# Deeper unit pipelines, a third value buffer and dense filler products in a one-step hybrid decoder kernel

## The chip, the cores and the metric

The kernel runs on one core of one Trainium2 chip. The metric is the device time of one execution in microseconds, the median over runs. All arithmetic is in float32 except mask products and fillers, which are bfloat16.

## The reference, cut to what matters

One layer of a hybrid decoder is applied to a prompt of 512 tokens and to 8 sample tokens, with the same weights:

```python
u = rmsnorm(x);  cols = u @ w_in                      # 1024 -> 4992, 13 slabs of 384 columns
# A: 6 heads, gated linear recurrence; the samples start from a given 64x64 state per head
# B: 6 heads, differential attention, 512 prompt keys / 512 cached + 1 keys per sample
p = softmax(mask(q @ k.T) * 32 ** -0.5);  o = (p[0] - lam * p[1]) @ v
# C: 3 groups of 4 heads, windows (128, 512, 2048) with strides (1, 4, 16); groups are
#    combined in proportion to their softmax denominators
mix = concat(readout_A(oa, silu(g)), readout_B(ob), combine_C(...))
h = x + mix @ w_out
h = h + hier_moe(rmsnorm(h))      # top group of 4, top 2 of its 4 experts; 16 experts, d_ff 512
h = h + sigmoid(rmsnorm(h) @ ple_w_gate) * (p_l @ ple_w_proj)
y = rmsnorm(h)
```

The new states, keys, values and window contents are outputs as well. The samples' cached keys and values of B lie in pages, found through a page table.

## The kernel before, in words

Each engine runs its own in-order program. Up to the output projection the programs are generated from one common list of steps, made by `schedule`; each engine executes, in the list's order, those steps that it has a function for. So a step's place in the list is its place in every engine's queue, the DMA queue of SyncE (SP) among them. Engines synchronise by counting semaphores.

The stages of the list, and where they lie in the profiled execution:

- **Projection and recurrence (17 to 239 us).** `proj` steps are pieces of the combined projection (L1967, L1972, L1975, L1978): a unit is 128 columns by 512 tokens ("FM"), or 128 tokens by 256 or 384 columns ("TM"), or the 8 samples ("SM", and "SS", which sums its four partial rows). A unit is cut in 4 pieces of 2 of the 8 contraction chunks (8 x 128). Units alternate between PSUM banks 0 and 1, weight slabs between two buffers. `weave` puts pieces behind the TensorE steps of the recurrence, 1.6 for each.
- **Sample state (239 to 267 us).** Eight `dst_v` steps: TensorE broadcasts a sample's value row to 128 partitions (L2188, contraction over 8 rows), VectorE multiplies it (L1604). Pieces are woven in at 0.3 for each, four more follow, then `dst_o` (L2197).
- **Differential attention (267 to 460 us).** 24 units (4 query tiles, 6 heads), each with three steps: `d_s(n)` makes two score maps in PSUM (L2049, mask L2052), VectorE takes the maximum (L1459), ScalarE exponentiates (L993); VectorE's `weigh` forms p0 - lam p1 (L1471 to L1474); `d_t(n)` transposes (L2064) and ScalarE copies (L1003); `d_pv(n)` multiplies by the values (L2076). The list goes `d_s(n)`, `d_t(n-1)`, `d_pv(n-2)`: 72 steps. After each, 1.7 pieces of projection. Probabilities lie in two buffers, the halves of `wk`. On VectorE `d_s(n)` first weighs unit n-1 and then takes the maximum of n.
- **Cached keys.** `q_out` stores the samples' queries; `cached(b, 0)` loads sample b's keys and its query, broadcast, into one of two buffers; GpSimd multiplies them (L786 to L788); `dec_q(b)` on VectorE sums (L1544 to L1547). The first comes 11 steps after `q_out`, then one every 5. `dec_new` (L1520 to L1539) prepares selection masks and the scores of the new rows.
- **Dilated attention (460 to 546 us).** 16 units, again score (L2094, mask L2096), maximum (L1482), exponential (L1027), transposes (L2112, copy L1038), value products (L2133): `c_s(n)`, `c_t(n-1)`, `c_pv(n-2)`, 48 steps. Four dense bfloat16 products of 128x256 (L2107, `BUSY`), whose result is overwritten, go ahead of each unit's transposes. The eight "res" units store their result and softmax statistics through DRAM to reorder rows; the merge on VectorE (L1496 to L1510) needs them back. No projection piece is left here. Beside these steps, one by one: `gate_fn` (a Silu on ScalarE with two table loads, L955), `dec_soft` and `dec_norm` (softmax of the samples), `krows` 0 to 3 (key rows transposed L2151, copied to two staging buffers L1060, stored by GpSimd), `dec_wt`, `gate_mul` (L1375), 16 `dec_v` steps (products of a sample's weights with its cached values: L2216 and L2211, then VectorE L1592 and L1588), and the read-outs `ro(i)` (L1654 to L1659, with ScalarE L1081 and L1082 between). `cached(b, 1)` loads values into the same two buffers as the keys, and waits until the products of sample b-2 are done.
- **Tail of the list (546 to 556 us)**: sums over samples, `mt` transposes.
- **Output projection and routing (556 to 660 us).** `wout` (L2292), `logits` (L2312); then VectorE finds groups, experts, and places of tokens, with small matmuls between (L2374 to L2378 for ranks, L2383 for the token lists). `pproducts` (L2364) are two early tiles of the last projection, put among them. The first gather of rows (L840) waits for the list.
- **Experts (658 to 1016 us)**, at least 16 tiles of 128 tokens in a loop (L2393, L2399, L2423), **and the last stage**.

The lines that set the order in question:

```python
D_SHARE = 1.7
Q_LAG, Q_EVERY = 11, 5
BUSY = 4
RO_EVERY = 10
weave([("dst_v", b) for b in range(NS)] + [("dst_new",)], 0.3)
```

## Time and profile before

| | us |
|---|---|
| median of 3 runs (lowest, highest) | 1104.04 (1103.67, 1109.15) |
| the profiled execution's own time | 1108.18 |
| its span, first to last instruction | 1106.4 |
| TensorE (PE) matmul busy | 1039.1 (94%) |
| VectorE (DVE) busy | 367.7 (33%) |
| ScalarE (ACT) busy | 249.1 (23%) |
| GpSimd (POOL) busy | 91.1 (8%) |
| mean granted TensorE clock | 0.964 |
| read from and written to HBM | 191.97 MB, 41.14 MB |

PE is the matmul part of TensorE, PEld its weight loads, which overlap. The ends of matmuls are modelled, so busy time says where TensorE was occupied, not how well. A granted clock of 1.00 is 2.4 GHz, 0.5 is 1.2 GHz; a value between is a mean over a stretch. SPq, POOLq and ACTq are the issuing of DMAs. "Ended last" means the chain of instructions followed back from the last one, at each step to what released it. "L1474" is line 1474 of the kernel.

### The profile page before, as it was taken

What the parts mean: (1) busy time and instruction counts of PE and PEld (TensorE: products, weight loads), DVE (VectorE), ACT (ScalarE), POOL (GpSimd) and SP (SyncE); (2) the same over time, 40 slices, a digit from 0 to 9 for tenths busy, and PEclk for the clock granted to TensorE, in tenths of its full rate; (3) what the DMA queues carried; (4) which work ended last, traced back from release to release, by engine and by line L of the source; (5) the groups of instructions that cost most, each with busy time, mean ns of one, the idle gap of its engine ahead of it and who ended that gap; (6) DMA issues with size and microseconds to landing.
All of it is one profiled execution on the core that took longest, in us unless ns stands there. A gap on an engine that the chain in (4) does not pass through costs nothing.

```text
span 1106.4 us, 11357 instructions
## 1 busy us (share of the span) xinstructions
PE 1039.1 (94%) x4147; PEld 542.3 (49%) x4147; DVE 367.7 (33%) x766; ACT 249.1 (23%) x577; POOL 91.1 (8%) x113
## 2 busy tenths in 40 slices
PE   6998999999998999888899969999999999998896
PEld 3444455544454765564644544444444444444342
DVE  5017436533225557255631341111011110100453
ACT  3043222211222322442421110001000100011454
POOL 1000000000005342010010010000000000001200
PEclk9998999988999999989999969999999999999999
DMA  6735303304346462346353285689998999886401
GB/s 200 285 133 162 131 3 133 133 3 164 133 139 230 153 212 61 113 154 198 122 199 123 77 318 194 241 305 343 350 345 305 343 348 341 286 330 250 134 20 57
DMA packets 97099, 214.92 MB, mean 194 GB/s; under 512 B 14481, under 2 KB 42996, under 8 KB 96668
## 3 DMA queue, kind: packets, MB, share of 16 engines
q1 hardware_dynamic: 86288, 185.78, 47.9%
q0 software_dynamic: 5616, 19.89, 5.0%
q10 hardware_dynamic: 5148, 8.63, 2.1%
q8 instruction: 28, 0.46, 0.2%
q14 instruction: 19, 0.16, 0.0%
HBM read 191.97 MB, written 41.14 MB: 211 GB/s over the span
## 4 chain that ended last, share of the span: by engine, by line
PE 81%; DVE 7%; DMA 3%; ACT 3%; SPq 2%; issue 2%; POOL 1%; ACTq 0%; DVEq 0%; POOLq 0%
PE ps L1967 15%; PE ps L2393 10%; PE ps L2423 10%; PE ps L2399 10%; PE ps L1972 7%; PE ps L2292 5%; PE ps L2488 5%; PE ps L2262 2%; PE ps L2003 2%; PE ps L1975 2%; PE ps L2049 1%; PE ps L2076 1%; PE ps L2188 1%; PE ps L1978 1%; SPq L636 1%
## 5 line engine op out<-in xcount | busy, mean ns | idle before, releaser
L1967 PE MATMUL ps<-xT,EXPERT 128*128 128x512 f32 x384 | 184.1, 623 | 1.5 <-DVE EXPERT L1298 1.5
L1972 PE MATMUL ps<-EXPERT,xT 128*128 128x384 f32 (+1 forms) x384 | 119.6, 454 | 0.0
L2393 PE MATMUL ps<-EXPERT,aF 128*128 128x512 f32 x256 | 114.7, 601 | 1.3 <-DVE aF L1856 1.3
L2423 PE MATMUL ps<-EXPERT,dF 128*128 128x512 f32 x256 | 112.6, 593 | 1.6 <-ACT dF L1171 1.6
L2399 PE MATMUL ps<-EXPERT,aF 128*128 128x512 f32 x256 | 112.5, 592 | 0.0
L1967 PEld LDWEIGHTS ps<-xT,EXPERT 128*128 128x128 f32 x384 | 71.3, 197 | 82.2 <-issue 79.0
L1972 PEld LDWEIGHTS ps<-EXPERT,xT 128*128 128x128 f32 x384 | 78.1, 237 | 25.6 <-issue 3.6
L2393 PEld LDWEIGHTS ps<-EXPERT,aF 128*128 128x128 f32 x256 | 49.4, 193 | 63.8 <-issue 62.1
L2423 PEld LDWEIGHTS ps<-EXPERT,dF 128*128 128x128 f32 x256 | 48.6, 190 | 62.6 <-issue 60.7
L2399 PEld LDWEIGHTS ps<-EXPERT,aF 128*128 128x128 f32 x256 | 47.4, 190 | 53.6 <-issue 53.6
L2488 PE MATMUL ps<-EXPERT 128*128 128x512 f32 x128 | 56.0, 594 | 2.7 <-DVE EXPERT L1913 2.7
L2292 PE MATMUL ps<-EXPERT,xT 128*128 128x512 f32 x128 | 57.2, 597 | 0.6 <-ACT xT L1087 0.6
L1856 DVE TENSOR_TENSOR aF<-ps,gains 128x1024 f32<-128x1024 f32 x16 | 19.6, 1223 | 113.4 <-PE ps L2262 113.4
L1175 ACT ACTIVATE wk<-ps 128x512 f32<-128x512 f32 x16 | 9.6, 597 | 204.8 <-PE ps L2423 204.8
L1862 DVE TENSOR_TENSOR dF<-dF,ps 128x512 f32<-128x512 f32 x16 | 11.0, 686 | 105.4 <-PE ps L2399 105.4
L993 ACT ACTIVATE wk<-ps,small 128x128 f32<-128x128 f32 (+3 forms) x48 | 24.9, 523 | 88.4 <-DVE small L1459 88.4
L1868 DVE COPY wk<-ps 128x512 f32<-128x512 f32 x16 | 11.1, 692 | 100.8 <-PE ps L2423 100.8
L1459 DVE TENSOR_REDUCE small<-ps 128x2 f32<-128x256 f32 (+3 forms) x24 | 19.7, 822 | 69.4 <-PE ps L2052 69.4
L929 ACT ACTIVATE EXPERT<-ps 128x384 f32<-128x384 f32 (+2 forms) x43 | 21.0, 489 | 90.6 <-PE ps L1967 47.4
L786 POOL TENSOR_TENSOR aF<-aF 128x1536 f32<-128x1536 f32 x4 | 14.1, 3527 | 320.6 <-DMA aF<-q_d 320.6
L2488 PEld LDWEIGHTS ps<-EXPERT 128*128 128x128 f32 x128 | 23.9, 190 | 31.4 <-issue 29.8
L2292 PEld LDWEIGHTS ps<-EXPERT,xT 128*128 128x128 f32 x128 | 23.5, 190 | 27.6 <-issue 27.5
(431 smaller groups left out, 1174.3 us busy)
## 6 DMA issues: line engine op xcount, KB each, us to landing
EXPERT<-in_moe_w_gate SPq DMA_DIRECT2D x16, 2048.0 KB, 15.1
EXPERT<-in_moe_w_up SPq DMA_DIRECT2D x16, 2048.0 KB, 20.0
EXPERT<-in_moe_w_down SPq DMA_DIRECT2D x16, 2048.0 KB, 10.0
EXPERT<-in_w_in SPq DMA_DIRECT2D x13, 1536.0 KB, 6.8
out_win_sample<-in_cache_win SPq DMA_DIRECT2D x16, 1022.0 KB
Yd<-wk ACTq DMA_DIRECT2D x16, 512.0 KB, 8.4
aF<-in_cache_k_diff SPq DMA_DIRECT2D x32, 192.0 KB, 2.5
aF<-in_cache_v_diff SPq DMA_DIRECT2D x32, 192.0 KB, 2.5
```

The lines of the kernel that those rows point to most:

```text
L929: s.activation(dst, src, ACT.Copy, scale=scale).then_inc(S_["unit_ok"], 1)
L993: last = s.activation(wk[:, n % 2, m * SEQ:m * SEQ + K], ps[:, 2 + 2 * (n % 2) + m, 0:K], ACT.Exp, bias=negm[:, 2 * (n % 2) + m:2 * (n % 2 ...
L1967: last = t.matmul(ps[:, u % 2, :], W_[:, c, c0:c0 + w], xT[:, c, 0:SEQ], start=(c == 0), stop=(c == DC - 1))
L1972: last = t.matmul(ps[:, u % 2, 0:w], rows_, W_[:, c, c0:c0 + w], start=(c == 0), stop=(c == DC - 1))
L1975: last = t.matmul(ps[32 * (c % 4):32 * (c % 4) + 32, u % 2, 0:w], xS[:, c, :], W_[:, c, :], start=(c < 4), stop=(c >= 4))
L2003: last = t.matmul(ps[:, 2 + 2 * (k % 2) + e, c * P:(c + 1) * P], L[h, c, :], R[h, c, :], start=True, stop=True)
L2262: last = t.transpose(ps[:, bank + c // 4, (c % 4) * P:(c % 4) * P + r], src[0:r, c * P:(c + 1) * P], ident[0:r, 0:r])
L2292: last = t.matmul(ps[:, 2 + 2 * (p % 2) + hf, :], xT[:, c, i * P:(i + 1) * P], wout_[c][:, hf * 512:(hf + 1) * 512], start=(c == 0), stop= ...
L2393: last = t.matmul(ps[:, 2 + 2 * b, :], xgT[b][:, c, :], wg_[b][:, c, :], start=(c == 0), stop=(c == DC - 1))
L2399: last = t.matmul(ps[:, 3 + 2 * b, :], xgT[b][:, c, :], wu_[b][:, c, :], start=(c == 0), stop=(c == DC - 1))
L2423: last = t.matmul(ps[:, 6 + hf, :], hT[b][:, c, :], wd_[b][:, c, hf * 512:(hf + 1) * 512], start=(c == 0), stop=(c == FC - 1))
L2488: last = t.matmul(ps[:, 4 + 2 * (p % 2) + h, :], hnT[p % 2][:, c, :], ple_[:, c, h * 512:(h + 1) * 512], start=(c == 0), stop=(c == DC - 1))
```

## The change

`schedule` and the constants:

```diff
-D_SHARE = 1.7
+D_SHARE = 1.5
+C_SHARE = 2
-Q_LAG, Q_EVERY = 11, 5
+Q_LAG, Q_EVERY = 16, 4
-BUSY = 4
-RO_EVERY = 10
+BUSY = 3
-    weave([("dst_v", b) for b in range(NS)] + [("dst_new",)], 0.3)
+    weave([("dst_v", b) for b in range(NS)] + [("dst_new",)], 1.0)
-    for n in range(nd + 2):
+    for n in range(nd + 3):
-        if 1 <= n <= nd:
-            d.append(("d_t", n - 1))
-        if n >= 2:
-            d.append(("d_pv", n - 2))
+        if 2 <= n < nd + 2:
+            d.append(("d_t", n - 2))
+        if n >= 3:
+            d.append(("d_pv", n - 3))
...
-    side = [("dec_soft",), ("krows", 0), ("dec_norm",)] + [("krows", u) for u in range(1, KR_EARLY)] + [("dec_wt",)]
-    side += [("dec_v", u) for u in range(2 * NS)]
+    side = [("krows", u) for u in range(KR_EARLY)] + [("dec_wt",)] + [("dec_v", u) for u in range(2 * NS)]
+    beside = {("dec_v", 1): ("gate_fn",), ("dec_v", 3): ("gate_mul",)}
+    beside.update({("dec_v", 5 + 3 * i): ("ro", i) for i in range(NT)})
...
+        if fresh == 2 and todo[0][0] > summed[10] + 1:
+            fresh = 1
+            steps.append(("dec_pre",))
+        if fresh == 1 and todo[0][0] > summed[12]:
+            fresh = 0
             steps.append(("dec_new",))
...
+        if st == ("d_pv", nd - 2):
+            steps.append(("dec_soft",))
...
     for k, st in enumerate(c):
         steps.append(st)
+        if k == 1:
+            steps.append(("dec_norm",))
         if todo:
-            project_one()
...
+            for _ in range(min(C_SHARE, len(todo))):
+                project_one()
+            if not todo:
+                steps += [("cached", 2, 1), ("outputs",)]
+                free = k + 1
+        elif side and k >= free:
+            free = k + C_PACE.get(beside_units(), 1)
```

The dilated steps get the same two-unit lag (`c_t(n-2)`, `c_pv(n-3)`). `beside_units` takes the next step of `side`, adds the one that `beside` names for it, and behind the last `dec_v` of sample b puts `cached(b+3, 1)`; the loads of the rest of `w_out` (`w_rest`, `w_more`) are placed there too.

Buffers and waits:

```diff
+        dP = [wrow[:, k * 2 * SEQ:(k + 1) * 2 * SEQ] for k in range(3)]
+        cP = [wk[:, 0, 0:SEQ], wk[:, 1, 0:SEQ], wk[:, 0, SEQ:2 * SEQ]]
+        kv3 = EXPERT[:, DC * SLAB:DC * SLAB + PAGES * SLAB]
+        vpage = kpage + [kv3.rearrange("p (j n) -> p j n", j=PAGES)]
+        kst = [wk[:, k, 2 * SEQ:3 * SEQ] for k in range(2)] + [EXPERT[:, 6 * D - SEQ:6 * D], wk[:, 1, SEQ:2 * SEQ]]
...
             def cached(b, kv):
-                buf, ld = b % 2, kvload[b % 2]
+                buf = b % 3 if kv else b % 2
...
+                elif kv == 1 and b == 2:
+                    sp.wait_ge(S_["unit_pe"], NU)
                 elif kv == 1:
-                    sp.wait_ge(S_["pv_pe"], 2 * (b - 1))
+                    sp.wait_ge(S_["pv_pe"], 2 * (b - 2))
...
             def d_s(n):                      # VectorE
-                if n:
-                    weigh(n - 1)
...
                                 AX.X, ALU.max, negate=True).then_inc(S_["d_max"], 1)
+                if n:
+                    weigh(n - 1)
...
-                    pool.dma_start(res_d.rearrange("(s r) n -> r s n", r=4)[x], resid[:, x]).then_inc(S_["res_st"], 16)
+                    pool.dma_start(to[:, 0:256], resid[:, x]).then_inc(S_["res_st"], 16)
+                    pool.dma_start(to[:, 256:CW], rst[:, x]).then_inc(S_["res_st"], 16)
```

`dec_new` is split: `dec_pre` has all but the third group's new row, which stays in `dec_new`. The samples' scores (`dec_soft`) are made in PSUM banks 2 and 3 instead of 0 and 1, the dilated scores start in banks 4 and 5, and `c_s(1)` waits until VectorE has read the samples' scores. The SM units of late slabs get a buffer of their own (`spart`).

TensorE, dilated stage and routing:

```diff
+            def dense(bank, count):
+
+                for _ in range(count):
+                    t.matmul(ps[:, bank, 0:2 * P], identb[:], mband[:], start=True, stop=True)
...
-                for _ in range(BUSY):
-                    t.matmul(ps[:, 6, 0:2 * P], identb[:], mband[:], start=True, stop=True)
+                dense(6, BUSY if n >= 4 else 0)
...
             columns_of(4)
+            dense(4, 8)
             logits(4)
...
             pproducts(0)
+            pproducts(1, (0,))
 
             pe.wait_ge(S_["c_ok"], T5 + 1)
...
-            pproducts(1)
+            pproducts(1, (1,))
+            dense(2, 20)
             pe.wait_ge(S_["rank_ok"], 1)
...
+            dense(3, 44)
             pe.wait_ge(S_["list_ok"], 1)
```

## Rows read from the trace of the kernel before

**Rows 1.** the page, part 4: shares of the chain that ended last, by engine.
```profile
PE 81%; DVE 7%; DMA 3%; ACT 3%; SPq 2%; issue 2%; POOL 1%; ACTq 0%; DVEq 0%; POOLq 0%
```

**Rows 2.** stretches: length, busy PE, PEld, DVE, ACT, POOL, granted clock, DMA share, GB/s.
```profile
239.40:266.55 27.15, 26.88 (x136) 11.54 (x135) 10.05 (x23) 1.67 (x3) 0.00 (x0) 0.69 0.51 169
266.55:459.60 193.05, 187.32 (x819) 111.17 (x816) 84.23 (x166) 53.19 (x158) 45.81 (x26) 0.99 0.41 136
459.60:486.60 27.00, 20.09 (x147) 15.67 (x146) 15.29 (x36) 15.73 (x39) 4.94 (x9) 0.77 0.63 217
486.60:545.80 59.20, 52.36 (x391) 32.95 (x394) 33.73 (x90) 20.70 (x72) 3.13 (x5) 0.93 0.50 153
625.60:639.04 13.44, 11.41 (x40) 6.49 (x38) 7.74 (x22) 2.90 (x7) 0.00 (x0) 0.75 0.60 199
639.04:647.69 8.65, 5.83 (x29) 3.56 (x27) 5.70 (x20) 2.25 (x4) 0.00 (x0) 1.00 1.05 401
647.69:657.73 10.04, 4.00 (x21) 3.91 (x21) 3.37 (x21) 1.28 (x1) 2.40 (x4) 0.53 0.91 345
657.73:670.08 12.35, 11.03 (x24) 5.42 (x25) 1.23 (x1) 0.00 (x0) 1.15 (x2) 0.69 0.22 73
```

**Rows 3.** waits of PE: engine, line, releaser: us in total, times, longest.
```profile
PE ps L2064 <- DVE wk L1474: 5.7, 2, 3.5
PE ps L2216 <- DMA EXPERT<-in_cache_win: 5.0, 5, 1.7
```

**Rows 4.** chain between 440 and 560 us: start, us, engine, tile, line, count.
```profile
449.91 0.77 PE ps L1975 x4
...
454.30 5.36 PE ps L1972 x16
...
488.04 1.03 PE ps L2133 x8
489.08 0.65 PE ps L2094 x8
489.72 0.32 PE ps L2096 x2
490.05 1.11 PE ps L2211 x6
...
524.24 0.44 PE ps L2107 x4
524.68 0.44 PE ps L2112 x4
525.11 0.78 PE ps L2216 x8
```

**Rows 5.** timeline of 222 to 270 us, PE: start, us, line, form, count.
```profile
241.25 2.39 PE L2188 MATMUL ps<-samp,ident 8*128 8x384 f32 x4 [0.27 <-DVE wk L1604]
```

**Rows 6.** timeline of 328 to 356 us, VectorE.
```profile
340.36 1.75 DVE L1544 TENSOR_REDUCE EXPERT<-aF 128x48 f32<-128x1536 f32 x1 [3.22 <-POOL EXPERT L788]
...
343.38 1.89 DVE L1473 TENSOR_SCALAR wk<-wk,small 128x256 f32<-128x256 f32 x1
...
348.80 0.35 DVE L1473 TENSOR_SCALAR wk<-wk,small 128x256 f32<-128x256 f32 x1
```

**Rows 7.** chain between 440 and 560 us, ScalarE.
```profile
464.46 1.80 ACT EXPERT L955
```

**Rows 8.** chain between 440 and 560 us, VectorE: one read-out, one merge.
```profile
528.53 0.96 DVE aF L1654
...
533.44 0.08 DVE fst L1496
...
535.39 0.86 DVE XM L1510 x4
```

**Rows 9.** timeline of 618 to 676 us, PE: the second early product.
```profile
641.19 3.68 PE L2364 MATMUL ps<-EXPERT 128*128 128x512 f32 x8
```

**Rows 10.** chain between 640 and 662 us: the first gather.
```profile
653.20 4.39 DMA aF<-u2d,samp
```

More of the change, by code:

```diff
@@ L228, in schedule @@
             at_q = k + Q_EVERY
-        if fresh and (not todo or todo[0][0] > summed[12]):
-            fresh = False
-            steps.append(("dec_new",))
-    project(stop - 1)
-    for _, b in keys:
-        steps += [("dec_q", b), ("cached", b + 2, 0) if b + 2 < NS else ("cached", b + 2 - NS, 1)]
-    if fresh:
-        steps.append(("dec_new",))
-    free, ro, n_ro, owed, open_ = 0, 0, 0, 0, True
+        if fresh == 2 and todo[0][0] > summed[10] + 1:
+            fresh = 1
+            steps.append(("dec_pre",))
@@ new lines, in schedule, with beside_units @@
+        if fresh == 1 and todo[0][0] > summed[12]:
+            fresh = 0
+            steps.append(("dec_new",))
+        if st == ("d_t", nd - 2):
+            steps += [("dec_q", b) for _, b in keys] + [("cached", b + 2 - NS, 1) for _, b in keys]
+            keys = []
+        if st == ("d_pv", nd - 2):
+            steps.append(("dec_soft",))
+    assert not fresh and todo
+    def beside_units():
+        kind = side.pop(0)
+        steps.append(kind)
+        if kind[0] == "dec_v" and kind[1] % 2:
+            b = kind[1] // 2
+            if b + 3 < NS:
+                steps.append(("cached", b + 3, 1))
+            if b + 4 == NS:
+                steps.append(("w_rest",))
+            if b == 3 * (NS // 3) - 1:
+                steps.append(("w_more",))
+        if kind in beside:
+            steps.append(beside.pop(kind))
+        return kind[0]
@@ L238, in schedule @@
+    free = 0
     for k, st in enumerate(c):
         steps.append(st)
+        if k == 1:
+            steps.append(("dec_norm",))
         if todo:
[L241 to L251 removed]
@@ L252, in schedule @@
-        if side and not todo and k >= free:
-            steps.append(side.pop(0))
-            kind = steps[-1]
-            if kind[0] == "dec_v" and kind[1] % 2 and kind[1] // 2 + 2 < NS:
-                steps.append(("cached", kind[1] // 2 + 2, 1))
-            free = k + C_PACE.get(kind[0], 1)
-    for kind in side:
-        steps.append(kind)
-        if kind[0] == "dec_v" and kind[1] % 2 and kind[1] // 2 + 2 < NS:
-            steps.append(("cached", kind[1] // 2 + 2, 1))
+            for _ in range(min(C_SHARE, len(todo))):
+                project_one()
@@ L262, in schedule @@
+            if not todo:
[3 more added lines that the diff above has]
+            free = k + C_PACE.get(beside_units(), 1)
+    while side:
+        beside_units()
     steps.append(("dec_out",))
-    steps += [("ro", i) for i in range(n_ro, NT)]
     late = [("krows", u) for u in range(KR_EARLY, n_kr)]
@@ L562, in hybrid_kernel @@
         KPER = 2 * PAGES // 2 + NG
+        V3_LOADS = 16 * KPER * len([b for b in range(NS) if b % 3 == 2])
         Q_STORES = 16 * 10
@@ L662, in outputs, with w_rest, w_more @@
                             out(rows_, cvT[:, g, i])
-            does = dict(slab=load_slab, copy=copy, state_in=state_in, state_out=state_out, q_out=q_out, cached=cached,
+            def w_rest():
+                wo = a["w_out"][0].rearrange("(c p) n -> p c n", p=P)
+                sp.wait_ge(S_["c_s_pe"], NCU // 2)
+                sp.wait_ge(S_["kr_pe"], KR_EARLY)
+                for c in range(WO_NOW, DC):
+                    sp.dma_start(wout_[c], wo[:, c]).then_inc(S_["woload_last"], 16)
+            def w_more():
+                sp.wait_ge(S_["pv_pe"], 2 * (LAST3 + 1))
+                wo = a["w_out"][0].rearrange("(c p) n -> p c n", p=P)
+                sp.dma_start(EXPERT[:, WO_FIRST * D:WO_NOW * D].rearrange("p (c n) -> p c n", c=WO_NOW - WO_FIRST),
+                             wo[:, WO_FIRST:WO_NOW]).then_inc(S_["woload"], 16)
+            does = dict(w_more=w_more, w_rest=w_rest, slab=load_slab, copy=copy, state_in=state_in, state_out=state_out, q_out=q_out, cached=cached,
                         outputs=outputs)
@@ L795, in krows @@
                 i, groups = KU[u]
-                stage = kst[u >= KR_EARLY][u % 2]
+                stage = kst[u]
                 pool.wait_ge(S_["kr_ok"], u + 1)
@@ L2361, in pproducts @@
                     pe.wait_ge(S_["pp_o"], i - 1)
-                for hf in range(2):
+                for hf in halves:
                     for c in range(PC):
```

173 lines of the change are left out of this document (88 added, 85 removed).

## The prediction

> **What bounds the kernel now.** I read the chain that ended last first, to see which engine carries the span: TensorE has 81% of it, no other engine over 7% [rows 1]. So the time is TensorE's own work, plus the stretches in which it waits, plus the stretches in which its granted clock is at 1.2 GHz in place of 2.4. An edit can win only by taking away one of the last two, or work. Next come the stretches, one for each stage the diff touches [rows 2]. For each, three numbers count: length, TensorE's busy time (the difference is waiting) and the granted clock, of which 1 minus it, times the length, is about what running at half clock costs. Sample state 27.15 us, waiting 0.3, clock 0.69: 8.4 us lost. Differential stage 193.05, waiting 5.7, clock 0.99: 1.9. First part of the dilated stage 27.00, waiting 6.9, clock 0.77: 6.2. Its second part 59.20, waiting 6.8, clock 0.93: 4.1. Routing: 13.44 at 0.75; 8.65 with 2.8 of waiting; 10.04 with 6.0 of waiting, at 0.53; 12.35 at 0.69. Nearly all of the rest (input, recurrence, experts, last stage) isn't touched. Then the waits themselves: 5.7 us on VectorE's weighing of probabilities, 5.0 on cached values [rows 3]. About 65 us are thus at stake in 1106.4.
>
> **The change part by part.** Total projection work stays the same; it only moves: a piece woven in elsewhere costs what it saves where it came from. I use the full-clock durations of rows 4 throughout.
>
> *Sample state (share 0.3 to 1.0).* Eight broadcasts of sample values, 8 rows deep, follow each other here with two pieces between them. The clock is low from about 242 to 259 though TensorE hardly waits: four of these matmuls took 2.39 us there [rows 5]. With eight pieces, each broadcast pair is followed by dense 128-row work. The six extra pieces are subtracted again from the differential stage. If the clock holds, 8.4 us go; nothing is late next, since VectorE is busy for only 10.05 of the 27.15 us [rows 2]. If it falls all the same, nothing changes: 0 to 8.4. I take 8.0, because the recurrence before it, with 1.6 pieces for each step, holds the clock.
>
> *Differential stage (lag of two, three buffers, 1.5 pieces for each step, cache keys later, preparation of the new rows split).* The 5.7 us of waiting [rows 3] are two events: 3.5 us at 343, where VectorE stood until GpSimd had multiplied the first cached keys and then ran a 0.35 us scaling in 1.89 us beside GpSimd [rows 6], and 2.2 us at 431 behind some 20 small instructions for the new rows. The first sum over keys moves from step 28 to 31 counted from the stage's start, and the queries go out at step 15 and not 17: five steps of some 2.6 us (193.05 / 72), or 13 us, of lead more, where VectorE stood for 3.22. TensorE's transposes now also need weights that are one unit older. Both waits should go, with the 1.9 us of clock: up to 7.6, at least 3; I take 7.0. The counter-load: key sums come every 4 steps, not 5, and VectorE (84 of 193 us busy) must do the same 84 in about 165, 51%. It holds if the lock of the next sentence stays rare.
>
> The rows show 1.89 against 0.35 us for the same scaling [rows 6]. The Trainium skill (SBUF — State Buffer, "SBUF: two separate sides") says why: the port pair that VectorE and GpSimd share is an exclusive lock, held for a whole instruction. The trace agrees. By that rule each of eight GpSimd products may hold a weighing up once, some 1.5 us, and the closer spacing makes it likelier; the sum above leaves it out because the older weights give one unit (7 us) of slack.
>
> *Dilated stage, start.* Of the 120 pieces left at the differential stage's start (126 from slab position 38 on, less six), 72 steps at 1.5 take 108; twelve move into the dilated stage, two a step: seven row pieces at 1.34 (a quarter of 5.36), four sample pieces at 0.77, one sum, 13.2 us [rows 4]. So the differential stage loses 13.2. The first part before is 27.00, of which 6.9 waiting, 6.2 clock and 12 dense products at 0.11 (1.3) are no work: 12.6 remain. The new rows' scores (1.3) go ahead into the differential stage. After: 12.6 + 13.2 - 1.3 = 24.5 if nothing waits. What made it wait is taken out: the gate's Silu of 1.80 us [rows 7] and the two table loads of 1.28 around it, 4.4 us of ScalarE, go behind the second value broadcast, the key rows have four staging buffers and no longer wait for the stores of the two before. I allow 3.7 us of leftover waits: 28.2, a gain of 12.0 over both stages. Bounds: 8 (waits of 7.7 stay) to 15.7 (none).
>
> *Dilated stage, values.* Waiting 6.8, clock 4.1, and 16 dense products fewer (52 to 36 here), 1.8: at most 12.7, a floor of 46.5. Waits for value loads are 5.0 us in five times, the longest 1.7 [rows 3]; a third buffer starts each load a whole sample, some 7 us, earlier, so that wait should not survive. VectorE is late next. The four read-outs (4.6 us each: from its first row to the merge's, less 0.33 of another product) [rows 8] stood at steps 6, 16, 26 and 36 of 48; now at 23, 29, 35 and 41, among the four merges (2.8 each). In the last 25 steps VectorE has 4 x 4.6 + 4 x 2.8 + 6 x 0.69 + 11 x 0.5 = 39.2 us, TensorE by rows 4: 5.8 of scores, 6.2 of transposes with 3 dense products, 9.5 of value products, 10.7 of broadcasts, 32.2 us. So these steps go at VectorE's pace: about 40 with its short waits, with 14 before them: 54, a gain of 5. Bounds: 12.7, and -3 if each read-out stalls the scores behind it in turn.
>
> *New waits.* The moved Silu holds ScalarE 4.4 us in the middle, where a unit takes 4.2 (54 / 13) and ScalarE's own share of it is 1.6 (20.70 / 13): 4.4 + 1.6 - 4.2, about 2 us. Residue statistics leave in a second store, and the read back must wait for both: 1 us. Together -3.0, bounds 0 and -6.
>
> *Routing.* Half of a projection product (of 3.68 us at full clock, less the tail: 1.7) [rows 9] now stands before the rank products, whose input was ready before TensorE came to them: +1.7. Behind them the other half and twenty dense products (2.2) take the place of the whole, 3.9 for 3.4, and 2.8 us of waiting stand there [rows 2]: free. Forty-four (4.8, at half clock 9.7) stand in the 6.0 us of waiting for the first gather, which itself took 4.39 [rows 10]. If they keep the clock up, the first expert products gain 3.8 (0.31 x 12.35), and I give the list products half of the 1.9 that half of their 4.0 us would be. -3.8 - 0.9 + 1.7 = a gain of 3.0. Bounds: 9 (the fall at 625 to 639 gone as well, 3.4) and -5.3 (1.7, and 9.7 in a hole of 6.0).
>
> **Sum.** 8.0 + 7.0 + 12.0 + 5.0 - 3.0 + 3.0 = 32.0 us. The profiled execution took 1108.18 us around its span of 1106.4, 4.1 over the median 1104.04. So: 1076.2 for a profile, 1072.0 for the median.
>
> **Rivals.** (a) *The clock does not hold*: the sample state keeps its 0.69 and the long run of dense products starts at half clock and ends behind the gather. Loses 8.0 and 3.0 + 5.3: gain 15.7, 1088.3. For it: at 239 to 243 the clock fell without idle time, so fullness alone is not what keeps it. Against: the six pieces are just the kind of work of the stages at 1.00. (b) *VectorE paces both attention stages*: values at 62 us (-8) and only 3 won in the differential stage (-4): gain 20, 1084.0. For it: 39.2 against 32.2 us; against: older weights. (c) *Everything hides*: values at 48 and full routing (+6, +4): 1062. (d) *Slower*: the dilated stage runs at half clock because each of its units keeps three dense products and the first four none. The stage holds about 24.5 + 46.5 us of TensorE work; every us of it at half clock costs 1. It decides from 32 us, under half of the stage; at 40 us the time is 1112. For it: part one, with four in each, shows 0.77. Against it: that part had 6.9 us of waiting, part two, with four as well, holds 0.93, and the twelve pieces stand where the fall was.
>
> **Chances.** A measurement of this kernel can't tell less than 0.5% (5.5 us) from no change. Forecast 0.41, (a) 0.20, (b) 0.17, (c) 0.13, (d) 0.09. Faster 0.85, within 0.5% 0.06 (the tail of (a) and (b) together), slower 0.09. The bounds add up to gains of 53.4 and of -3.3; the likeliest case alone spans 1065 to 1080, and the range that leaves two in ten out is 1057 to 1096.
>
> **What would show it.** Right: granted clock over 0.95 while sample values are broadcast; no wait on the weighing line over 1 us; no wait for cached values; TensorE's waits in the last third of the dilated stage naming VectorE; first expert products in about 7 us, not 9.26. Wrong: a clock of 0.5 to 0.7 in the sample state (a), waits on the weighing that are longer than before (b), a clock under 0.8 through the dilated stage (d).

## The result, and the profile after

Over interleaved runs the changed kernel took 1096.85 us (median of 11, 1093.01 to 1100.41), the kernel before 1104.95 us (median of 11, 1100.56 to 1112.06). The ratio is 0.991, 95% interval 0.9888 to 0.9931: faster by 0.9%, some 10 us. Forecast were 32 us and a median of 1072.0; the range went from 1057 to 1096, and the median lies just outside it. The direction came, a third of the size came.

The profiled execution took 1093.97 us around a span of 1092.2, against 1108.18 around 1106.4 before: 14.2 us less. The median of the ratio is worth only 10. Part of the 14.2 is luck: the profiled execution before lies 3.2 us above its kernel's median, the one after 2.9 us below. The page of the kernel after, parts 1 and 4 (busy time of the engines, then the chain that ended last):

```profile
span 1092.2 us, 11449 instructions
...
PE 1036.8 (95%) x4191; PEld 541.4 (50%) x4191; DVE 384.0 (35%) x766; ACT 248.1 (23%) x577; POOL 95.0 (9%) x117
...
PE 81%; DVE 9%; ACT 3%; SPq 2%; DMA 2%; issue 2%; POOL 1%; ACTq 0%; DVEq 0%; POOLq 0%
```

TensorE still carries the span; VectorE's share of the chain went from 7% [rows 1] to 9%. The stretches of the kernel after follow, in the columns of [rows 2]: sample state, differential stage, dilated start, dilated values, up to the first output product, first expert products. The differential stage ends here where the first dilated score starts, since pieces of projection follow behind that score. By the same cut the kernel before has 193.8 and 26.3 us in place of the 193.05 and 27.00 of [rows 2]; its line stands first:

```profile
266.50:460.30 193.80, 188.07 (x822) 111.25 (x816) 84.23 (x166) 53.68 (x159) 45.81 (x26) 0.99 0.41 135
```
```profile
239.40:267.20 27.80, 27.80 (x160) 11.48 (x160) 10.05 (x23) 2.27 (x4) 0.00 (x0) 1.00 0.44 151
267.20:442.40 175.20, 169.60 (x765) 104.58 (x763) 102.96 (x172) 50.90 (x156) 47.60 (x26) 0.98 0.46 152
442.40:469.70 27.30, 26.92 (x189) 17.02 (x188) 7.26 (x24) 13.50 (x41) 5.44 (x10) 1.00 0.25 76
469.70:531.10 61.40, 53.02 (x348) 31.70 (x347) 39.23 (x96) 23.56 (x70) 4.72 (x8) 0.84 0.63 210
531.10:543.06 11.96, 11.33 (x83) 6.64 (x83) 5.37 (x13) 5.79 (x9) 1.65 (x3) 0.82 0.40 126
...
647.50:656.30 8.80, 8.80 (x18) 3.82 (x19) 0.00 (x0) 0.00 (x0) 0.78 (x1) 0.81 0.20 60
```

Set against the forecast, stage by stage (us; the forecast column is the prediction's own terms put onto the column before; the last two rows are distances between first instructions):

| stage | before | forecast | after | miss |
|---|---|---|---|---|
| sample state | 27.15 | 25.75 | 27.80 | +2.05 |
| differential | 193.8 | 167.0 | 175.2 | +8.2 |
| dilated, start | 26.3 | 27.5 | 27.3 | -0.2 |
| dilated, values | 59.20 | 57.20 | 61.40 | +4.20 |
| to the first output product | 9.81 | 9.81 | 11.96 | +2.15 |
| output, routing, to the first expert product | 105.37 | 102.37 | 104.42 | +2.05 |

They add up to 18.5; the rest of the kernel is 0.7 shorter, which leaves the 17.8 between 32.0 and 14.2. The largest miss by far, 8.2, is the differential stage. What TensorE waited for in the kernel after (total, times, longest), to be laid beside [rows 3]:

```profile
PE ps L2112 <- ACT PT L1041: 5.6, 1, 5.6
PE ps L2002 <- ACT PT L1076: 4.6, 4, 1.7
PE ps L2265 <- DMA EXPERT<-in_cache_win: 2.4, 1, 2.4
PE ps L2436 <- DVE samp L1867: 2.4, 1, 2.4
PE ps L2181 <- DVE XM L1548: 1.4, 3, 0.7
```

Before, 5.7 us of waiting in the differential stage were two waits; now 5.6 us are one. The releaser is called ScalarE (a copy that stood behind a late exponential), but the cause is on VectorE. Its timeline around the wait in the kernel after (start, us, what, forms, idle time ahead of it):

```profile
381.82 2.18 DVE L1511 TENSOR_SCALAR wk<-wk,small 128x384 f32<-128x384 f32 x1
384.04 1.50 DVE L1512 SCALAR_TENSOR_TENSOR wk<-wk,small 128x384 f32<-128x384 f32 x1
386.15 1.75 DVE L1587 TENSOR_REDUCE EXPERT<-aF 128x48 f32<-128x1536 f32 x1 [0.61 <-POOL EXPERT L824]
...
388.74 0.30 DVE L1559 TENSOR_REDUCE EXPERT<-ident 96x12 f32<-96x96 f32 x1
...
392.87 2.87 DVE L1577 TENSOR_TENSOR EXPERT<-EXPERT,ident 8x32 f32<-8x32 f32 x1
...
397.88 1.22 DVE L1495 TENSOR_REDUCE small<-ps 128x2 f32<-128x1024 f32 x1
```

A weighing that takes 0.42 and 0.62 us undisturbed takes 2.18 and 1.50 beside GpSimd. Then come the sum over the sixth sample's keys (386.15) and directly behind it the preparation of the new rows, some 20 small instructions (388.74 to 397.85), one of which, 8 rows by 32 elements, takes 2.87 us in place of 0.18. Only after them does the next unit's maximum start (397.88). From the last weighing's end (385.5) to that maximum VectorE did nothing for the units for 12.3 us, when a unit takes 7.3 (175.2 / 24); the one unit of slack was gone.

### The profile page after: what moved, and what is told of

The parts are those of the page before. It is cut to its first block, busy times and chain, and to the rows that moved or that the text cites. A ratio compares the mean times of both kernels' runs of the same rounds, so it can differ in the third digit from the quotient of the medians.

```text
span 1092.2 us, 11449 instructions
## 1 busy us (share of the span) xinstructions
PE 1036.8 (95%) x4191; PEld 541.4 (50%) x4191; DVE 384.0 (35%) x766; ACT 248.1 (23%) x577; POOL 95.0 (9%) x117
## 4 chain that ended last, share of the span: by engine, by line
PE 81%; DVE 9%; ACT 3%; SPq 2%; DMA 2%; issue 2%; POOL 1%; ACTq 0%; DVEq 0%; POOLq 0%
PE ps L2015 15%; PE ps L2446 10%; PE ps L2476 10%; PE ps L2452 10%; PE ps L2020 7%; PE ps L2341 5%; PE ps L2542 5%; PE ps L2051 2%; PE ps L2311 2%; PE ps L2023 2%; PE ps L2097 1%; SPq L608 1%; PE ps L2124 1%; PE ps L2361 1%; PE ps L2026 1%
## 5 line engine op out<-in xcount | busy, mean ns | idle before, releaser
L2015 PE MATMUL ps<-xT,EXPERT 128*128 128x512 f32 x384 | 180.6, 612 | 1.5 <-DVE EXPERT L1336 1.5
L2341 PE MATMUL ps<-EXPERT,xT 128*128 128x512 f32 x128 | 57.2, 597 | 0.6 <-ACT xT L1125 0.6
L1905 DVE TENSOR_TENSOR dF<-dF,ps 128x512 f32<-128x512 f32 x16 | 11.0, 688 | 105.4 <-PE ps L2452 105.4
L1495 DVE TENSOR_REDUCE small<-ps 128x2 f32<-128x256 f32 (+3 forms) x24 | 19.7, 822 | 54.3 <-PE ps L2100 54.1
L2341 PEld LDWEIGHTS ps<-EXPERT,xT 128*128 128x128 f32 x128 | 23.5, 190 | 27.6 <-issue 27.5
```

The lines of the kernel that those rows point to most:

```text
L2015: last = t.matmul(ps[:, u % 2, :], W_[:, c, c0:c0 + w], xT[:, c, 0:SEQ], start=(c == 0), stop=(c == DC - 1))
L2341: last = t.matmul(ps[:, 2 + 2 * (p % 2) + hf, :], xT[:, c, i * P:(i + 1) * P], wout_[c][:, hf * 512:(hf + 1) * 512], start=(c == 0), stop= ...
```

## The experiments

All ratios are to the kernel before, with 95% intervals. Unless said otherwise an experiment starts from the changed kernel (0.991).

**1. The sample state's share alone, in the kernel before.**

```
-    weave([("dst_v", b) for b in range(NS)] + [("dst_new",)], 0.3)
+    weave([("dst_v", b) for b in range(NS)] + [("dst_new",)], 1.0)
```

> The kernel before with the sample state's share of projection pieces raised from 0.3 to 1.0 and nothing else. Theory: the six pieces moved there (8.1 us of TensorE work in the changed kernel's trace) leave the differential stage, and the clock no longer falls while the sample values are broadcast: the stretch takes 27.8 in place of 27.15 us, the differential stage 8 us less, so 7 us less in all, ratio 0.993 to 0.995. Rival, that a fall of the clock which is avoided here comes back in a later stage whatever one does: under 2 us, ratio 0.998 to 1.001, with a low stretch more in the differential stage.

Measured 0.9974 (0.9944 to 1.0005), 1102.17 us. Its profile has a span of 1099.6, 6.8 less than before. Sample state and differential stage (193.8 in the kernel before):

```profile
239.30:267.20 27.90, 27.90 (x161) 11.54 (x160) 10.06 (x23) 2.27 (x4) 0.00 (x0) 1.00 0.43 150
267.20:452.70 185.50, 180.23 (x796) 107.77 (x794) 87.49 (x166) 52.33 (x158) 46.02 (x26) 0.99 0.44 143
```

The clock holds (1.00, before 0.69 [rows 2]), the differential stage is 8.3 shorter, and the profile gives the 7 of the theory; the ratio gives 3, and its interval ends just short of 0.994 and just past 1. The mechanism is shown, its size in the median is not.

**2. New rows prepared late.**

```
-        if fresh == 2 and todo[0][0] > summed[10] + 1:
+        if fresh == 2 and not keys and k >= at_q - 2:
```

> The changed kernel with the 20-odd small instructions that prepare the new rows put three steps behind the last sum over cached keys, not right behind the sixth. Theory: the 5.6 us wait for transposed weights at 393 us and the low clock behind it (6.8 us at 0.5, 3.4 us) come from these instructions standing, between two key sums, in front of one unit's maximum: both go, 7 to 9 us under the changed kernel, ratio to the kernel before 0.983 to 0.986. Rival, that VectorE is full there (37.7 of 46 us busy between 340 and 386 us) and only the place of the stall is chosen by the new rows: a wait of 3 us or more appears at another unit and the gain is under 3 us, ratio 0.988 to 0.992.

Measured 0.985 (0.9813 to 0.9887), 1088.92 us: by the ratios 6.6 us under the changed kernel. The wait on the weighing:

```profile
PE ps L2112 <- DVE wk L1512: 1.9, 1, 1.9
```

1.9 in place of 5.6. The ratio lies in the theory's range; its 7 to 9 us were just missed, and the rival's 3 were passed. The place of the 20 instructions counted, and something besides was left.

**3. Half of the prompt's value stores behind the fourth sample's loads.**

```
-            def outputs():
+            def outputs(part=0):
...
+                for i in ((0, 1), (2, 3))[part]:
+                    prompt_rows(i)
...
                 steps.append(("cached", b + 3, 1))
+            if b == 0:
+                steps.append(("outputs", 1))
```

> The changed kernel with half of SyncE's stores of prompt values (rows of the last two tiles) put behind the load of the fourth sample's cached values, in place of all of them ahead of it. Theory: the load was issued at 480.3 us, though its buffer was free by 476, only since 14 us of stores stood ahead of it on SyncE's queue; the 2.4 us wait at 486 goes, and with it the low clock from 487 to 498 (10.2 us at 0.5, 5 us): 5 to 7 us under the changed kernel, ratio 0.985 to 0.987. Rival, VectorE sets the pace of the whole dilated stage: the wait goes and appears as a wait for VectorE or ScalarE within three steps, gain under 2 us, ratio 0.989 to 0.992.

Measured 0.9904 (0.987 to 0.9938), 1095.60 us: nothing won. Its waits, and the issue on SyncE's queue of the load that was now late:

```profile
PE ps L2121 <- DVE wk L1521: 10.6, 1, 10.6
...
PE ps L2274 <- DMA EXPERT<-in_cache_win: 1.8, 1, 1.8
```
```profile
490.74 3.64 SPq L666 DMA_DIRECT2D aF<-in_cache_v_diff  x4
```

The fourth sample's values came in time, the fifth's did not: its issue stood behind the half of the stores that had been put off, and the wait of 1.8 came at 496 us. So the waits fit the queue theory, with too few stores moved (experiment 6 moves all), though the ratio lies in the rival's range; the rival's sign (VectorE instead) was not seen. And the first line is news: a wait of 10.6 us in a differential stage in which nothing had been changed against the kernel after, whose profile shows 5.6.

**4. Routing as before.**

```
-            dense(4, 8)
-            pproducts(1, (0,))
-            pproducts(1, (1,))
-            dense(2, 20)
+            pproducts(1)
-            dense(3, 44)
```

> The changed kernel without the dense products in the routing waits (8, 20 and 44) and with the second projection product whole behind the rank products, as before. Theory: they are worth about what the trace shows between the first output product and the first expert product, 1 us: ratio 0.991 to 0.993, the first expert products take 8.8 us or more, and the hole before the gather shows 5 to 6 us again. Rival 1, the prediction's: they are worth 3 us or more, ratio 0.994 or over. Rival 2: their half-clock work in front of the expert rows costs more than it keeps: ratio 0.989 or under.

Measured 0.9941 (0.9913 to 0.9969), 1098.01 us: by the medians' ratios 3 us over the changed kernel, but the intervals overlap. The ratio itself lies just inside rival 1's range. The distance from the first output product to the first expert product is the better measure: 105.4 (before), 104.4 (experiment 1), 105.9 here, so 105.2 on average without the dense products, against 104.4 to 105.2 in the eleven profiles with them, 104.8 on average. There they are worth 0.4 us, less than the spread of either group, not 3.0. The gather's hole is back at 6.2 us, as the theory had it. The rest of this profile's loss sits elsewhere: 6.4 us in the differential stage and 4.8 from the first expert product on. That the dense products have no part in the latter is not shown. Its differential stage, and VectorE in front of the sixth key sum:

```profile
267.50:449.10 181.60, 170.24 (x765) 104.88 (x761) 103.43 (x172) 50.74 (x156) 47.15 (x26) 0.96 0.44 146
```
```profile
389.61 1.75 DVE L1587 TENSOR_REDUCE EXPERT<-aF 128x48 f32<-128x1536 f32 x1 [5.22 <-POOL EXPERT L824]
```

11.4 us of waiting (181.60 less 170.24) in a stage whose code is that of the changed kernel. VectorE stood 5.22 us in front of the key sum because GpSimd was late, and GpSimd because its keys were. How long keys take shows in the kernel after, for the fifth sample: SyncE issued the loads (361.45 to 367.06) and GpSimd started when they had landed:

```profile
361.45 3.62 SPq L664 DMA_DIRECT2D aF<-in_cache_k_diff  x4
...
366.64 0.42 SPq L671 DMA_DIRECT2D aF<-q_d  x1
```
```profile
371.87 3.44 POOL L822 TENSOR_TENSOR aF<-aF 128x1536 f32<-128x1536 f32 x1 [6.30 <-DMA aF<-q_d]
```

A key buffer's round is 5.6 us of issue, 4.8 of landing, 5.9 of products and some 3.4 until VectorE has summed and SyncE issues again: 19.7 us, or 9.8 for each sample with two buffers (the same buffer's products start at 352.24, 371.87 and 391.98). Four steps of the schedule last 4 x 175.2 / 72 = 9.7 with the stall in them and 9.3 without (167.5, below). The schedule asked for keys faster than the buffers turn. Before, five steps lasted 13.5.

**5. Key sums every five steps.**

```
-Q_LAG, Q_EVERY = 16, 4
+Q_LAG, Q_EVERY = 16, 5
```

> The changed kernel with the sums over cached keys every five steps again, in place of four; the preparation of the new rows stays where its projection pieces put it. Theory, from the four traces with sums every four steps: a key buffer's round (5.4 us of issue on SyncE, landing, 5.9 us of GpSimd's products, 2.9 us of VectorE's sum) lets one sample through each 10 us or so, the schedule asks for one each 9.6; VectorE, which works in order, stands before a sum until GpSimd is through (5.2 us idle in one trace) and the weighing behind it is late. At five steps, 12 us, the round keeps up: the waits for weighed probabilities fall from 5.6 to 11 us to under 3, 5 to 8 us under the changed kernel, ratio 0.984 to 0.987. Rival: only the adjacency of new rows and key sum counts; they still follow each other closely, so 0.989 to 0.992.

Measured 0.9865 (0.984 to 0.989), 1091.5 us: by the ratios 5 us under the changed kernel, in the theory's range (the two intervals just touch). The differential stage, and two VectorE instructions of it, the fifth key sum and one of the new rows' behind it:

```profile
266.20:434.10 167.90, 167.84 (x767) 103.09 (x763) 95.26 (x172) 50.80 (x156) 46.84 (x26) 1.00 0.48 158
```
```profile
379.82 1.74 DVE L1587 TENSOR_REDUCE EXPERT<-aF 128x48 f32<-128x1536 f32 x1
...
387.62 2.87 DVE L1577 TENSOR_TENSOR EXPERT<-EXPERT,ident 8x32 f32<-8x32 f32 x1
```

The waits are gone to the last tenth, the clock is at 1.00, VectorE is 7.7 us less busy for the same instructions (fewer of them stretched), and the stage is 7.3 us shorter than the 175.2. The new rows still stand directly behind a key sum, and one of them is still stretched to 2.87 us: so the rival, that only this adjacency counts, is out. The 7.3 us are the forecast's 7.0 of the differential stage, got by one figure of the schedule.

**6. New rows late, all prompt value stores last.** As experiment 3, with all of the prompt's rows behind the last value load and the last output weights (`steps.append(("outputs", 1))` behind `("w_rest",)`), on top of experiment 2.

> The kernel of the second experiment (new rows prepared late) and with all of the prompt's value stores put behind the last load of cached values and of output weights. Theory: value loads are late only by SyncE's queue: no wait for cached values above 0.5 us is left, the 2.5 us of the second experiment go with the low clock behind it: 3 to 6 us under that experiment, ratio 0.980 to 0.982. Rival, VectorE paces: the same time comes back as waits for weights, maxima or merges: ratio 0.984 to 0.987.

Measured 0.9837 (0.9818 to 0.9857), 1089.08 us, between the two ranges. The dilated stage, from its first score up to the transposes behind the sums over samples (93.1 us at a clock of 0.87 in the kernel after), of experiment 2, then of this one:

```profile
438.10:531.80 93.70, 85.10 (x566) 50.38 (x565) 47.45 (x124) 37.08 (x111) 10.17 (x18) 0.85 0.49 160
```
```profile
440.00:528.30 88.30, 78.07 (x567) 46.99 (x566) 47.23 (x124) 36.82 (x111) 10.16 (x18) 0.94 0.54 169
```

No wait for cached values is left, and the stage is 5.4 us shorter: not by waiting (8.6 in experiment 2, 10.2 now: it came back as waits for merges and copies), but by the clock, 0.85 to 0.94 (1 less the clock, times the length: 14.1 and 5.3 us). Of that the median ratio shows 1.4 us, inside the error.

**7. New rows late, read-outs three value products earlier.**

```
-    beside = {("dec_v", 1): ("gate_fn",), ("dec_v", 3): ("gate_mul",)}
-    beside.update({("dec_v", 5 + 3 * i): ("ro", i) for i in range(NT)})
+    beside = {("dec_wt",): ("gate_fn",), ("dec_v", 1): ("gate_mul",)}
+    beside.update({("dec_v", 2 + 3 * i): ("ro", i) for i in range(NT)})
```

> The kernel of the second experiment with the four read-outs, the gate's product and its Silu three value products earlier, so that the last read-out ends a fifth of the stage sooner. Theory of the prediction: VectorE paces the last third of the dilated stage (39.2 against 32.2 us); spread over more steps it does not: the 6 us of waits that name VectorE and ScalarE there fall to 3, ratio 0.979 to 0.983, 2 to 5 us under the second experiment. Rival: those waits come from the order of single instructions, not from the load; they move to the middle with the read-outs, ratio 0.984 to 0.987, or worse if the Silu now holds ScalarE where the dilated stage starts.

Measured 0.9858 (0.9837 to 0.988), 1092.22 us: no gain on experiment 2. The wait that goes back to VectorE's maxima through ScalarE's copies:

```profile
PE ps L2002 <- ACT PT L1076: 8.1, 5, 2.3
```

2.2 us in experiment 2, 8.1 here. The longest, 2.3 us at 468 us, is the Silu's, which holds ScalarE from 465.8 to 470.2 with its table loads; another of 1.5 at 482 stands behind the first read-out. The ratio lies in the rival's range, and the waits moved as it said: a read-out stands in front of a unit's maximum, wherever it is put. Spreading the load of the last third did not help.

**8. New rows late, four dense products for every unit.**

```
-BUSY = 3
+BUSY = 4
-                dense(6, BUSY if n >= 4 else 0)
+                dense(6, BUSY)
```

> The kernel of the second experiment with four dense products ahead of every unit's transposes in the dilated stage, the first four units too (28 dense products more, 3 us at 0.11). Theory: they stand where TensorE has no idle time in the first part and fill waits in the second, and the clock of that stage (0.84 in the changed kernel's values part) rises: between -4 and +1 us against the second experiment, ratio 0.982 to 0.986. Rival, the prediction's slower case turned round (the clock is lost because the number of dense products is too small): 5 us or more gained, under 0.981. Second rival, they cost what they take: +3 us, 0.988.

Measured 0.9845 (0.9818 to 0.9872), 1089.71 us. The dilated stage:

```profile
441.00:529.60 88.60, 79.64 (x594) 48.65 (x593) 47.59 (x124) 37.47 (x111) 10.16 (x18) 0.96 0.53 169
```

28 dense products more, and 5.1 us shorter than in experiment 2, at a clock of 0.96 against 0.85; there are still 9.0 us of waits. In the medians nothing of it can be told from noise (the ratio lies in the theory's range).

Why do 5 us of the dilated stage not show in experiments 6 and 8? Their profiles don't show them over the whole span either: 1087.6 us in experiment 2, 1087.0 in 6, 1088.9 in 8. Experiment 6 lost 1.9 us in the differential stage, where a piece of projection now waits for ScalarE:

```profile
PE ps L2028 <- ACT EXPERT L975: 3.8, 1, 3.8
```

It lost 3.0 more from the first expert product to the end (446.1 us for 443.1), experiment 8 lost 2.3 before the differential stage, 0.6 in it and 3.7 in the experts. Most of this is in code that no edit touched: from the first expert product to the end the profiles of this study take between 443.1 and 449.5 us. A gain of 5 us in one stage of one profile is no larger than that.

**9. Keys of six samples not loaded.** The output's part for samples 2 to 7 is left out; queries, products and sums stay, and the counts of loads that GpSimd and TensorE wait for are adapted.

```
-                for j in range(PAGES):
+                for j in range(PAGES if kv or b < 2 else 0):
-                for g in range(NG):
+                for g in range(NG if kv or b < 2 else 0):
```

> The changed kernel, sums over cached keys every four steps, new rows prepared where it prepares them; the cached keys and window rows of samples 2 to 7 are not loaded (this part of the output is left out; the queries' copy still is loaded, and GpSimd multiplies and VectorE sums what stands in the buffers). Theory of the buffers' round: with the loads of 5.4 us of issue gone GpSimd is never late, VectorE no longer stands before a sum, and the wait of 5.6 to 11 us at some 393 us is under 2.5: ratio 0.984 to 0.987. Rival, the lock between VectorE and GpSimd (2 to 3.7 us for a weighing of 0.4 us) is what delays the weights: the products still run beside the weighing, the wait stays at 4 us or more, ratio 0.989 to 0.992.

Measured 0.9852 (0.9814 to 0.9891), 1090.64 us. The wait, and the worst of the new rows' instructions:

```profile
PE ps L2112 <- ACT PT L1041: 3.8, 1, 3.8
```
```profile
390.52 3.54 DVE L1575 TENSOR_TENSOR EXPERT<-samp 8x256 f32<-8x256 f32 x1
```

VectorE's longest wait for GpSimd is 0.61 us, and the time fell as the theory had it; but 3.8 us of TensorE's wait stayed, where the theory had under 2.5 and the rival 4 or more. It stands behind the new rows and one instruction of them that took 3.54 us beside a GpSimd product. The kernel after shows the same 0.61 us at this place (386.15, above), so nothing at this place shows that the other 1.8 us of its 5.6 are late keys. What had grown most on VectorE is the weighing. The same 48 instructions of the differential stage, in the kernel before and in the kernel after (busy us, mean ns | idle time ahead):

```profile
L1474 DVE SCALAR_TENSOR_TENSOR wk<-wk,small 128x128 f32<-128x128 f32 (+3 forms) x24 | 15.7, 653 | 0.9
...
L1473 DVE TENSOR_SCALAR wk<-wk,small 128x128 f32<-128x128 f32 (+3 forms) x24 | 13.9, 580 | 0.8
```
```profile
L1511 DVE TENSOR_SCALAR wk<-wk,small 128x128 f32<-128x128 f32 (+3 forms) x24 | 21.7, 904 | 0.8
L1512 DVE SCALAR_TENSOR_TENSOR wk<-wk,small 128x128 f32<-128x128 f32 (+3 forms) x24 | 21.7, 903 | 0.9
```

That is 29.6 us before and 43.4 after, while VectorE stood for late GpSimd 3.2 us in the stage before and 1.8 after. Experiment 2 has 44.1, experiment 5 has 36.3, experiment 9 has 37.8. So experiments 5 and 9 took away late keys and long weighings together, and how much each is worth is not shown. Shown is this: with the new rows elsewhere and the weighings as long as ever, 1.9 us of wait are left (experiment 2); with the new rows in place and the key sums five steps apart, none (experiment 5). The likely reading is that either load alone all but fits into the one unit of slack, and both together do not.

**10 to 12. Put together.** Experiment 10 is 2, 6 and 8 together; 11 is 10 with sums every five steps; 12 is 10 with the sample state's share back at 0.3.

> The three changes of the second, sixth and eighth experiments together: new rows prepared late, prompt value stores last, four dense products ahead of each unit's transposes. Theory: the low clock of the dilated stage (7 to 12 us in the changed kernel's traces) follows its waits; with the value waits gone and the short ones filled, what the profile loses to the clock between 440 and 545 us falls under 3 us: ratio 0.979 to 0.983. Rival: each removed the same loss, nothing adds up: 0.983 to 0.986.

> The kernel of the tenth experiment with the sums over cached keys every five steps and the new rows behind the last of them. Theory: the waits for weighed probabilities, under 2 us in the traces with late new rows, go altogether; -2 to +1 us against the tenth experiment, ratio 0.978 to 0.983. Rival: eight sums now end so late that the new rows and the scores of cached keys meet the differential stage's end: a wait of 3 us or more there, ratio 0.984 or over.

> The kernel of the tenth experiment with the sample state's share of pieces back at 0.3, six pieces more in the dilated stage's start. Theory: the clock falls again for 17 us while the sample values are broadcast, 8 us more there, and nothing gives it back: 5 to 8 us over the tenth experiment, ratio 0.986 to 0.990. Rival, as the first experiment's median leaves it open: the pieces do as much for the clock of the dilated stage as they did in the sample state; 0 to 3 us over the tenth, ratio 0.980 to 0.984.

Measured: 10: 0.9849 (0.9809 to 0.9888), 1090.39 us. 11: 0.9808 (0.9766 to 0.9849), 1084.2 us. 12: 1.0019 (0.9993 to 1.0045), 1109.86 us. Differential and dilated stage of 10, of 11, and of 12 with its sample state ahead of them:

```profile
267.80:441.00 173.20, 169.36 (x765) 103.90 (x761) 100.95 (x172) 50.73 (x156) 47.64 (x26) 0.99 0.47 154
441.00:531.80 90.80, 82.78 (x595) 50.68 (x594) 47.35 (x124) 37.28 (x111) 10.17 (x18) 0.92 0.52 165
```
```profile
266.20:433.70 167.50, 167.50 (x763) 103.12 (x761) 92.72 (x172) 50.98 (x156) 46.72 (x26) 1.00 0.48 159
433.70:524.00 90.30, 81.28 (x595) 50.11 (x594) 47.27 (x124) 37.29 (x111) 10.16 (x18) 0.94 0.53 166
```
```profile
238.30:265.40 27.10, 26.83 (x137) 11.50 (x136) 10.04 (x23) 1.67 (x3) 0.00 (x0) 0.69 0.51 169
265.40:446.80 181.40, 172.65 (x765) 104.30 (x763) 83.60 (x172) 51.16 (x156) 46.01 (x26) 0.97 0.44 144
446.80:552.10 105.30, 95.06 (x618) 57.63 (x617) 47.65 (x124) 37.96 (x112) 10.17 (x18) 0.89 0.44 142
```

Experiment 10 is in the rival's range: in the dilated stage the gains of late stores and of dense products, both of them clock, don't add up (90.8 us at 0.92, worse than either alone). Experiment 11 is in its theory's range and has the lowest time of the study, 11 us under the changed kernel by the ratios, though its interval overlaps those of experiments 2 and 5 to 10; its differential stage has no wait at all. Experiment 12 went far past both ranges: 19 us over experiment 10. The sample state loses its clock again (0.69), as forecast. But its 27.10 us, with 8 us less work in them, take about as long as the 27.8 of the kernel after; the time is lost behind it. Its waits between 239 and 600 us:

```profile
PE ps L2189 <- DVE XM L1556: 9.2, 2, 5.0
PE ps L2023 <- ACT EXPERT L975: 5.4, 1, 5.4
PE ps L2120 <- ACT PT L1049: 2.8, 1, 2.8
```

The differential stage is 8.2 us longer than in experiment 10: a piece waits 5.4 us for a copy by ScalarE, which stands behind an exponential that waits for VectorE. VectorE in turn stood for GpSimd, whose keys were late (VectorE's waits in this stage; 3.7 us in experiment 10):

```profile
DVE EXPERT L1595 <- POOL EXPERT L832: 11.0, 2, 5.6
```

The weighings are the shortest of all here, 27.5 us. So late keys alone can hold the units up too; in the kernel after they did not get that far. The dilated stage, with 18 pieces in its start, takes 14.5 us more: 8.3 are the six pieces, 2.2 more waiting, and about 4 the lower clock (0.89 against 0.92); the value broadcasts begin 16 us later and are squeezed among fewer units, and merges are waited for 9.2 us. I had expected 5 to 8 us, all of it the sample state's clock.

## Why the prediction was wrong

*What bounds the kernel.* Right: TensorE's work, waits and clock, and all differences lie there.

*Sample state, 8.0.* Right in mechanism: clock 1.00 in place of 0.69. The term counted the six pieces at 6.6 us; most of them are pieces of 128 columns by 512 tokens, 1.88 us each, 8.1 in all (15 matmuls of 512 columns at 0.48, and 0.9 of others). That is 1.5 of the 2.05 in the table; for the rest the clock gave back 7.5 (27.15 + 8.1 - 27.80), not 8.0.

*Differential stage, 7.0.* This is the step that failed. "Both waits should go": one of 5.6 us stayed in the profile, with 6.8 us at half clock from within it on, and waits of 10.6 and 10.7 in two others of the same stage. The prediction saw the counter-load ("key sums come every 4 steps, not 5"), but took it as a share of the whole stage ("must do the same 84 in about 165, 51%"), and put both it and the lock at nothing, because of one unit of slack. VectorE took 103 us for it, not 84 (172 instructions in place of 166), and 13.8 of the difference are in the weighings alone; between 340 and 386 us it was busy for 37.7 of 46 us (82%). And the distance of key sums was not held against the round of the key buffers (9.8 us a sample, where four steps last 9.3), though issue, landing, product and sum each had a row in the trace before. Experiment 5 gives the 7 us back by the spacing alone; experiment 2 takes 3.7 of the wait away, and 2.9 us of the stage, by the place of the new rows. How the rest divides between late keys and held-up weighings stays open.

The lock that the prediction named is real here, and hits small instructions as hard as large ones: 2.87 us in place of 0.18, from 392.87 to the end of the GpSimd product at 395.7. The Trainium skill (SBUF — State Buffer, "SBUF: two separate sides") has it as an exclusive lock for a whole instruction. The trace agrees.

The 18 pieces that left this stage were counted rightly, 19.8 for 20.0 measured (the four lines of projection matmuls are busy for 154.3 us in this stage before and for 134.3 after). But the sum has a slip: the 1.3 us of the new rows' scores were taken off the dilated stage and not put onto this one; they are 2.0 here.

*Dilated start, 12.0.* Its size came, 27.3 for 27.5, but by luck: of the 3.7 us allowed for waits only 0.4 came, and there were some 3 us more of work, 1 of them in the pieces (14.2, not 13.2).

*Dilated values, 5.0, and new waits, -3.0.* The stage got longer, 61.4, not 57.2. "That wait should not survive": one survived, 2.4 us, since the fourth sample's load stood behind 14 us of stores on SyncE's queue. A step's place in the list is its place in that queue too, and the prediction did not count it. Stores last, no wait (experiment 6). "These steps go at VectorE's pace" was right in what is seen, TensorE waiting for copies behind late maxima, 4.6 us; but spreading the read-outs did not help (experiment 7), so it is not the load of these steps that decides. And no term was set for the clock in a stage whose waits were to be small: it lost some 12 us up to the last sums (0.87 of 93.1), 10 before. A part of that is the 2.15 in the table's next row, where the clock was still low.

*Routing, 3.0.* The hole went as forecast (6.0 to 0.8 us of waiting before the gather), but the half clock in it had cost nothing, since all of the gather's wait stood in it. The clock fell once more at 648 us: the first expert products took 8.8 us, 3.4 of them at half clock, for 9.3 before, 4.3 of them at half clock. The list products took 3.98 us for 4.00, where 0.9 was forecast. The term priced a low clock over a stretch (0.31 x 12.35) under an "if they keep the clock up", and the dense products did not. As far as the profiles show they are worth 0.4 us (experiment 4).

*From profile to median.* The forecast took the profile's gain over unchanged. The changed kernel's profile met a 5.6 us stall, two others of the same stage 10.6 and 10.7, with 5 to 6 us more in that stage (180.6 and 181.6, against 175.2). Stages that no edit touched vary by as much (experiment 8). Which of these makes the 14 of the profile the 10 of the ratio is not shown.

*Rivals.* By time (a), 1088.3, was the nearest, but it did not come in the sample state, and in routing only in that the dense products started at half clock; they did not delay the gather. By mechanism (b), VectorE paces both attention stages (1084.0), was the nearest: its differential half came and more, its dilated half came through a queue and a clock. (d) was not reached (0.87, not under 0.8).

Still open: how the stall divides between late keys and held-up weighings, in the profiled executions and in the others; and why from the first expert product on some profiles take 6 us more than others.

## What to carry to other kernels

When work on a slow path is put closer together, hold the new distance against the round of its buffers (issue, landing, product, sum), and the busy time of the engine that serves them against the stretch in question, not against the whole stage; instructions that two engines hold each other up in get longer when they meet more often. One figure of the schedule, 4 for 5, cost a third of what the change could give. Put nothing long between the maximum of one unit and the next on the engine that serves them, and read the queue of the engine that issues a load before you credit a buffer. Pieces of work also hold a place in the order: six of them, 8 us of work, made 19 us when they stood in later stages.

## What the runs showed of the hardware

A VectorE instruction with two inputs, on 8 rows by 32 elements, took 2.87 us beside a GpSimd product, and 0.18 us alone; one of 8 by 256 took 3.54 and 0.41 (experiment 9), one of 96 by 1 took 3.08 and 0.15 (experiment 4). A VectorE reduction of 8 by 256 ran in its 0.41 us beside the same GpSimd product that had the 8 by 32 wait (392.43 us; the product from 391.98 to 395.7). The granted clock fell to 0.5, TensorE's 1.2 GHz, at TensorE's longer waits in the kernel after (398.9 to 405.7 us, from within the 5.6 us wait on; 487.6 to 497.8 us, from within the 2.4 us wait on), but not behind the waits of 1.7 and 1.4 us at 504 and 515 us; it fell from 521.7 to 535.4 behind the third of these short ones. Two edits of quite different kind, no value wait and four dense products in place of three, both raised the dilated stage's clock from 0.85 to 0.94 and 0.96, and together did not do more (0.92).
